# A first projection chunk computed as seven half-size products, and the modulation steps spread over other steps, in a fused two-block kernel

## The reference, cut to what matters

```python
def first_block(x, w_in, w_out, ...):
    u = einsum('bsd,de->bse', h, w_in[layer])          # 2048 -> 6752 columns
    q, k, v, z_attn, q_idx, k_idx, w_idx, z_ssd, xbc, dt_raw = _split_cols(u, IN_WIDTHS)
    ...                                                 # sparse attention, SSD mixer
    sub = einsum('bse,ed->bsd', mixed, w_out[layer])
    h = _layer_norm(DEEPNORM_ALPHA * h + sub, ln_g[layer], ln_b[layer])

def second_block(x, c, w_mod, b_mod, mod_layer, ...):
    mod = silu(c) @ w_mod + b_mod + mod_layer[l]        # one row times 2048 x 12288
    shift1, scale1, gate1, shift2, scale2, gate2 = split(mod, 6)
    ...                                                 # gating, attention, 32 experts
```

## Time and profile before

| | |
|---|---|
| median of 3 runs | 1990.54 us (1987.9 to 1991.35) |
| the profiled execution: its time, its span | 1994.43 us, 1992.7 us |
| PE busy | 1840.9 us (92%) |
| DVE busy | 1112.3 us (56%) |
| ACT, POOL busy | 321.4 us (16%), 180.4 us (9%) |
| mean granted TensorE clock | 0.984 of full |

### The profile page before, as it was taken

The page is one execution under the profiler, slowest core; times in us unless marked ns, Lnnn a source line. Parts: engine busy times, 40 slices in busy tenths (PEclk is TensorE's granted clock), DMA queues, the critical chain, the costliest instruction groups (busy, mean ns, idle before and its releaser), DMA issues.

```text
span 1992.7 us, 24068 instructions
## 1 busy us (share of the span) xinstructions
PE 1840.9 (92%) x9846; PEld 1425.9 (72%) x9846; DVE 1112.3 (56%) x1582; ACT 321.4 (16%) x607; POOL 180.4 (9%) x190
## 2 busy tenths in 40 slices
PE   8999999999999999999999999999959987788776
PEld 3788988888688788788888888868845554444443
DVE  3776677643688777767785754655463322232222
ACT  0111221221311232000241112411310000000000
POOL 0000041000000000000000000000002211111211
PEclk9999999999999999999999999999969999999999
DMA  9554532222223556568555751054299999999996
GB/s 349 184 186 154 178 122 75 79 65 84 85 85 127 192 188 242 210 232 299 185 183 201 252 192 64 22 206 169 107 376 400 409 403 403 415 404 402 413 418 242
DMA packets 153228, 448.42 MB, mean 225 GB/s; under 512 B 19446, under 2 KB 118108, under 8 KB 126748
## 3 DMA queue, kind: packets, MB, share of 16 engines
q1 hardware_dynamic: 122012, 305.92, 40.3%
q0 software_dynamic: 24288, 118.32, 17.1%
q10 hardware_dynamic: 6816, 22.60, 3.1%
HBM read 440.42 MB, written 26.28 MB: 234 GB/s over the span
## 4 chain that ended last, share of the span: by engine, by line
PE 38%; DMA 20%; DVE 3%; issue 1%; ACT 0%; POOL 0%; DVEq 0%; POOLq 0%; SPq 0%; ACTq 0%
PE bank L1184 20%; DMA RW<-in_gate_up 9%; PE bank L1213 7%; PE bank L1380 3%; DMA RA<-xn_d,dt_ 3%; DMA RX<-in_gate_up 2%; DMA RG<-in_down 2%; DMA RM<-in_down 2%; PE bank L1391 2%; PE bank L1121 1%; DMA out<-RA,dt_ 1%; PE bank L934 1%; DVE RG L1996 1%; PE bank L1007 1%; DMA RG<-in_w_mod 1%
## 5 line engine op out<-in xcount | busy, mean ns | idle before, releaser
L1184 PE MATMUL bank<-RW,RX 128*128 128x256 f32 x1792 | 404.0, 383 | 4.8 <-PE bank L1184 2.1
L1184 PEld LDWEIGHTS bank<-RW,RX 128*128 128x128 f32 x1792 | 341.7, 192 | 61.4 <-issue 14.8
L1996 DVE SCALAR_TENSOR_TENSOR RG<-RG,ccol 128x2048 f32<-128x2048 f32 x90 | 211.6, 2352 | 91.9 <-DMA RG<-in_w_mod 85.0
L1987 DVE TENSOR_TENSOR RW<-RW 128x2048 f32<-128x2048 f32 (+1 forms) x84 | 188.3, 2247 | 90.9 <-PE bank L1184 65.1
L1184 PE MATMUL bank<-RW,RM 128*128 128x256 f32 x1056 | 236.6, 380 | 1.5 <-PE bank L1184 1.2
L1184 PEld LDWEIGHTS bank<-RW,RM 128*128 128x128 f32 x1056 | 199.6, 190 | 32.1 <-issue 5.5
L2978 DVE TENSOR_TENSOR RA<-RA,bank 128x128 f32<-128x128 f32 x34 | 9.8, 288 | 282.8 <-ACT RA L1956 282.6
L1451 ACT ACTIVATE RA<-bank 128x512 f32<-128x512 f32 (+3 forms) x155 | 79.0, 538 | 539.6 <-PE bank L1184 273.3
L852 POOL DMA_DIRECT2D RG<-in_w_mod x96 | 51.3, 534 | 986.5 <-DVE RG L1996 598.9
L1184 PE MATMUL bank<-RX,RW 128*128 128x256 f32 x544 | 122.3, 379 | 0.3 <-PE bank L1184 0.3
L1184 PEld LDWEIGHTS bank<-RX,RW 128*128 128x128 f32 x544 | 102.2, 190 | 15.0 <-issue 1.6
(11 more groups left out here) (295 smaller groups left out, 2328.7 us busy)
## 6 DMA issues: line engine op xcount, KB each, us to landing
RG<-in_w_mod POOLq DMA_DIRECT2D x96, 1024.0 KB, 5.5
RW<-in_w_in SPq DMA_DIRECT2D x71, 1024.0 KB, 5.4
RX<-in_gate_up SPq DMA_DIRECT2D x22, 2048.0 KB, 42.1
RW<-in_gate_up SPq DMA_DIRECT2D x22, 2048.0 KB, 41.0
RG<-in_down SPq DMA_DIRECT2D x11, 2048.0 KB, 42.2
RM<-in_down SPq DMA_DIRECT2D x11, 2048.0 KB, 41.0
RM<-in_gate_up SPq DMA_DIRECT2D x10, 2048.0 KB, 42.4
RH<-in_gate_up SPq DMA_DIRECT2D x10, 2048.0 KB, 43.4
```

What stands on the lines that cost most here:

```text
L1184: ins = nc.tensor.matmul(bk[:, part], x, y, start=name not in ("M2", "M3") and k + j == 0, stop=k == half - 1, skip_group_check=True)
L1987: st.do(v.tensor_tensor(dst, x, y, op), s, n)
L1996: st.do(v.scalar_tensor_tensor(out=dst, in0=x, scalar=sc, in1=y, op0=op0, op1=op1), s, n)
```

## The change

Chunk 0 joins `FAST` and `project_first` goes. ACT issues all four parts of the input, by quadrants: tokens 0 to 255 of the first 4 and the next 4 blocks of features (A11), then tokens 256 to 511 of all 16 (A21 and A22, 2 MB, semaphore `x_later_tokens`), then A12. Each piece is now rows of 1 KB. DVE begins with `sum_first_input`: S1, the first weight sum of chunk 0, S2, S4, S3; its nine first mods go to later steps. The mods are distributed anew (24 before chunk 5 as before; 9, 8 and 7 in chunks 12, 13 and 14 in place of 10, 10 and 6; 6 at the end of chunk 18 in place of 4), and four of the vectors' sums on PE move: (2, 10), (12, 12), (14, 11) and (16, 11) become step 14 of the same chunk.

```diff
-        FAST_X, FAST_OUT = [1, 2, 3] + list(range(first["z"], first["za"] + 2)), [first["out"] + n for n in range(3)]
+        FAST_X, FAST_OUT = [0, 1, 2, 3] + list(range(first["z"], first["za"] + 2)), [first["out"] + n for n in range(3)]
...
-        MODS_AT = {(c, kt): 1 for c, steps in ((1, (7, 8, 9, 10, 12)), (2, (7, 8, 10, 12)), (3, (7, 8, 9, 10, 12, 13)),
-                                               (12, (0, 1, 2, 3, 4, 7, 9, 11, 13, 15)), (13, (0, 1, 2, 3, 4, 9, 10, 11, 13, 15)))
+        MODS_AT = {(c, kt): 1 for c, steps in ((0, (6, 7, 8, 9, 10, 12)), (1, (7, 8, 9, 10, 12, 13)), (2, (7, 8, 10, 12, 15)), (3, (7, 8, 9, 10, 11, 12, 13)),
+                                               (12, (0, 1, 2, 5, 7, 9, 11, 13, 15)), (13, (0, 1, 2, 3, 4, 9, 11, 13)), (14, (3, 6, 7, 9, 10, 11, 12)))
...
-        MODSUM_AT = {(2, 10): 0, (12, 12): 1, (14, 11): 2, (16, 11): 3, (19, 2): 4}
+        MODSUM_AT = {(2, 14): 0, (12, 14): 1, (14, 14): 2, (16, 14): 3, (19, 2): 4}
...
-                if n == 2:
-                    sp.dma_start(X[:, 8:KD, :], a["xt"][:, 8:KD, :]).then_inc(x_landed, 16)
...
-            act.dma_start(X[:, 0:4, :], a["xt"][:, 0:4, :]).then_inc(sem("x_first"), 16)
-            act.dma_start(X[:, 4:8, :], a["xt"][:, 4:8, :]).then_inc(sem("x_part"), 16)
+            act.dma_start(X[:, 0:4, 0:256], a["xt"][:, 0:4, 0:256]).then_inc(sem("x_first"), 16)
+            act.dma_start(X[:, 4:8, 0:256], a["xt"][:, 4:8, 0:256]).then_inc(sem("x_part"), 16)
+            act.dma_start(X[:, :, 256:S], a["xt"][:, :, 256:S]).then_inc(sem("x_later_tokens"), 16)
+            act.dma_start(X[:, 8:KD, 0:256], a["xt"][:, 8:KD, 0:256]).then_inc(x_landed, 16)
...
+            def sum_first_input():
+
+                dve.wait_ge(sem("x_later_tokens"), 16)
+                tt_(left(0, "S1"), left(0, "A21"), left(0, "A22"), ALU.add, sem("left_sums"))
+                dve.wait_ge(sem("x_first"), 32)
+                first_sum(0)
+                dve.wait_ge(sem("x_part"), 16)
+                dve.wait_ge(sem("left_sums"), 1)
+                tt_(left(0, "S2"), left(0, "S1"), left(0, "A11"), ALU.subtract, sem("left_sums"))
+                dve.wait_ge(x_landed, 16)
+                st.settle()
+                sum_left_rest(0)
+                dve.wait_ge(sem("csil_ready"), 1)
```

More of the change, by code:

```diff
@@ L466, in posts @@
             return []
-        MODS_AFTER_SUMS, MODS_AFTER_FIRST, MODS_AHEAD_OF_ROWS, MODS_BEHIND_ROWS = 7, 2, 2, 2
-        MODS_AT = {(c, kt): 1 for c, steps in ((1, (7, 8, 9, 10, 12)), (2, (7, 8, 10, 12)), (3, (7, 8, 9, 10, 12, 13)),
-                                               (12, (0, 1, 2, 3, 4, 7, 9, 11, 13, 15)), (13, (0, 1, 2, 3, 4, 9, 10, 11, 13, 15)))
+        MODS_AHEAD_OF_ROWS, MODS_BEHIND_ROWS = 2, 2
+        MODS_AT = {(c, kt): 1 for c, steps in ((0, (6, 7, 8, 9, 10, 12)), (1, (7, 8, 9, 10, 12, 13)), (2, (7, 8, 10, 12, 15)), (3, (7, 8, 9, 10, 11, 12, 13)),
+                                               (12, (0, 1, 2, 5, 7, 9, 11, 13, 15)), (13, (0, 1, 2, 3, 4, 9, 11, 13)), (14, (3, 6, 7, 9, 10, 11, 12)))
                    for kt in steps}
-        MODS_AT.update({(c, kt): 2 for c, steps in ((14, (7, 9, 12)), (15, (2, 7, 9, 12)), (16, (2, 7, 9, 12)), (19, (3, 7, 9, 12)), (20, (2, 7, 9, 12)))
+        MODS_AT.update({(c, kt): 2 for c, steps in ((15, (2, 7, 9, 12)), (16, (2, 7, 9, 12)), (19, (3, 7, 9, 12)), (20, (2, 7, 9, 12)))
                         for kt in steps})
-        MODS_AT.update({(18, 15): 4})
-        MODS_BEFORE_Z = MODS_AFTER_SUMS + MODS_AFTER_FIRST + sum(n for (c, _), n in MODS_AT.items() if c < Z_AT)
-        MODSUM_AT = {(2, 10): 0, (12, 12): 1, (14, 11): 2, (16, 11): 3, (19, 2): 4}
+        MODS_AT.update({(18, 15): 6})
+        MODS_BEFORE_Z = sum(n for (c, _), n in MODS_AT.items() if c < Z_AT)
+        MODSUM_AT = {(2, 14): 0, (12, 14): 1, (14, 14): 2, (16, 14): 3, (19, 2): 4}
         MODSUM_TILE = {}
@@ L1136, in project @@
                     beside(c, kt)
[L1138 to L1160, removed]
             def project_seven(c):
@@ L1173, in project_seven @@
                             pe.wait_ge(sem("sums_moved"), 2)
-                    if name in ("M1", "M2", "M3"):
+                    if (c, name) == (0, "M1"):
+                        pe.wait_ge(sem("x_first"), 32)
+                    elif name in ("M1", "M2", "M3"):
                         s, count = load_of[c, q]
                         pe.wait_ge(w_landed[s], count)
+                    if (c, name) == (0, "M2"):
+                        pe.wait_ge(x_landed, 16)
                     elif name in ("M5", "M6", "M7"):
@@ L1180, in project_seven @@
                     for k in range(half):
+                        if (c, name, k) == (0, "M1", 4):
+                            s, count = load_of[c, q]
+                            pe.wait_ge(sem("x_part"), 16)
+                            pe.wait_ge(w_landed[s], count)
                         for j in range(2):
@@ L1844, in stage @@
                         continue
+                    if c == 0:
+                        copy_product(c, "M1", raw(c, 0, 1))
+                        copy_product(c, "M5", raw(c, 1, 1))
                     if chunks[c][0] == "xbc" and c in FAST:
@@ L2815, in stage @@
                         mod_steps(MODS_AT.get((c, kt), 0))
-                    if c and c + 1 in FAST:
+                    if c + 1 in FAST:
                         first_sum(c + 1)
@@ L2830, in stage @@
                     elif chunks[c][0] == "xbc":
+                        if c == 0:
+                            take_pack()
                         work(c)
```

23 lines of the change are left out of this document (8 added, 15 removed).

## The result

The changed kernel takes 1994.32 us (median of 20 runs, 1989.48 to 1997.14) for 1989.99 us before (20 runs, 1987.65 to 1992.32): ratio 1.0020, interval 1.0014 to 1.0026. It is slower by about 4 us, where 2 us less were forecast. In a second comparison (12 runs beside 35 of before) the ratio was 1.0001, interval 0.9989 to 1.0012, which does not meet the first. Both together, each weighted by its interval, give about 3 us (an estimate). The profiled execution took 1992.22 us, span 1990.5, 2.2 us less than the profiled one of before. This pair points the other way because of its first member: the profiled execution of before, 1994.43 us, lies above every one of those 20 (of the 35 of the second comparison some reach 1996.18).

A forecast was written before the change was run, and what follows sets the result against it. PE's timeline was taken as the bound where the change works. Terms +1.5 - 3.1 + 1.0 + 0.9 - 3.7 + 0.6 + 1.0 gave -1.8, taken as -2 on 1994.43; less 3.9, 1988.5 us, range 1983 to 1994.5.

The forecast's parts named there:

- The base of the sum: Whole kernel: -2 us taken on the profiled 1994.43, then 3.9 taken off to reach the median of the runs: 1988.5.
- the zero for chunks 1 to 3: Chunks 1 to 3, one more mod each: no cost, with 0 to 2 us for chunk 3.
- Each stop of 1.79 us or more: PE's stops from chunk 12 on: each cost its own length and 1.7 us more through the halved clock.
- After 1.50 us of idling: PE's idling of 1.50 us, spread over more: no fall of the clock behind it, granted clock 1.00.
- Chunk 0: Start of the kernel: seven products save about 6.3 us, lost in the wait for later tokens; +1.5 us.
- Chunk 12: Chunk 12: -3.1 us from M3's stop, +1.0 for stops ahead of PV, +0.9 for clock falls behind them.
- Chunk 13 and the start of 14: Ahead of M5 of chunk 14: S1 comes earlier, saving the 2.04 us stop and 1.7 of clock; -3.7 us.
- The sums in chunks 14 and 16: PE's stops ahead of the vectors' sums: 3.3 us for 2.74 (+0.6) and 2.8 for 1.79 (+1.0).
- Rival (d): Chunk 12 stays bound by DVE's attention work, both new stops lower the clock; 1991 to 1992 us, chance 0.16.
- Rival (c): Chunk 0: later tokens land much later because quadrant rows run slower; at 250 GB/s +7, 1995.5 us; chance 0.12.
- Rival (b): Chunk 0's loads: 1 KB records run at full rate, -2.8 us more, 1985.7 us; chance 0.06.

The follow-up runs named there:

- chunk0_only: The changed kernel with the mods of chunks 12 to 18 and three of the four moved vector sums put back as before; 1995.69 us, ratio 1.0024.
- later_steps: The changed kernel with chunk 3's seventh mod at step 4, not 13, and the vector sums of chunks 14 and 16 at step 15; 1982.61 us, ratio 0.9970.
- sum_first: The changed kernel with DVE making chunk 0's first weight sum ahead of S1 instead of behind it; ratio 0.9993.
- before_again: The kernel before, without any edit, run and profiled a second time; ratio 1.0001.

## Why the prediction was wrong

**The base of the sum failed most, then the zero for chunks 1 to 3.** The step that failed most is "I take -2 on the profiled execution's 1994.43 ... That execution is 3.9 above the median". In the profiled execution all four stops of 1.79 us or more were followed by a fall of the clock, 6.8 us in all. The sum took two of those falls away as gains of the change (1.7 in chunk 12, 1.7 at the start of chunk 14), and then the 3.9 us by which the falls, in the main, had made that execution slow were taken off again: 3.4 us counted twice. "Each stop of 1.79 us or more here cost itself and 1.7 us" was read from one execution as if it were the program's. Over the profiles of all kernels here, of 14 stops of 2.53 to 3.14 us in chunks 12 to 16, 7 were followed by a fall; of 8 of 1.95 to 2.34 us, 5; of 22 of 1.72 to 1.86 us, 2. The place counts beside the length: of the 20 stops of 1.7 to 1.8 us ahead of PV one was followed by a fall, but the stop of 1.50 us ahead of chunk 18, with some 1.4 us more of idling in the 4 us behind it, was followed by one in 10 of 14 profiles, three times of 6.8 us. The prediction's "After 1.50 us of idling spread over more there was no such fall" was one execution's as well. A typical execution of before had less to give back. Its 35 runs in the second comparison say the same: the nine with a mean granted clock of 0.985 or more took 1989.0 us on average, the ten with 0.982 or less 1993.2. The Trainium skill (TensorE: Matmul & The Clock Gate, What's actually happening) says that the point at which the clock changes varies from run to run with the phase in which the first matmul lands; that the phase decides is not shown by any run here. What the profiles show is such a variation at stops in the middle of a kernel: the same stop of chunk 14 with a fall at 2.88 us in one execution and without at 2.58 in the next, and one of 3.14 us without in a third kernel.

Two more steps failed, in chunk 0 and in chunks 1 to 3. With all of them put right, the forecast's own sum is -1.8 + 3.4 (the falls counted twice) + 0.8 (chunk 0) + 1.8 (chunk 4) - 0.9 (falls in chunk 12 that did not come) = +3.3 us (an estimate), where the two comparisons together give about 3. That the profiled execution of the changed kernel took 1992.22 us, and the working had 1992.4 for it, is luck: it had falls behind both vectors' sums and behind the stop ahead of chunk 18.

**Chunk 0** (+1.5): +2.9 and +2.7 us in the two profiles of the changed kernel. With the same start chunk0_only has chunk 1 at 70.2 and later_steps at 69.2; the four average 70.3, the five profiles with the old start 68.0, which makes +2.3. So the term was 0.8 us too small. M1 at 6.6 (6.1 forecast) and the tokens near 21 (20.5) are 0.5 us late, which leaves M5 at 25.8 (25.3). The rest is the restart, which came out as 6.0, 5.6, 4.6 and 2.8 us at half rate, for 4.4. Two readings in the working are loose, without weight in the sum: by its own numbers seven products are 6.9 us less than eight, not 6.3, and two sums behind 20.5 end at 25.1, not 25.3. The record-for-record sharing of two queues was the right mechanism: from 12 to 18 us the DMA view has one record for one.

```profile
q10 hardware_dynamic: 1028, 1.05, 56.0%
q1 hardware_dynamic: 1029, 1.04, 54.2%
```

That the weight sum stands behind S1, for 2.2 us, was in the working, but not that it need not: sum_first shows it.

**Chunks 1 to 3** ("Zero, with 0 to 2 us for chunk 3, whose seventh mod stands ahead of the taking of M4"): the mechanism was named and the wrong end of its range taken. It costs 1.8 us (16.6 us for 14.7 from chunk 4's start to chunk 5's). The mods there go at the pace of their loads, and the sixth waited as long as any (3.27 us); moving one mod to step 4, as in later_steps, so that none stands at step 13, removes the stop.

**Chunk 12** (-3.1 +1.0 +0.9): the stops came as worked out, 0 ahead of M3, 1.83 for 1.8, 1.72 for 1.75. The +0.9 for falls behind the new stops was nearly nothing in fact: one fall behind the 20 stops of this kind in all kernels. Against before_again, which had no fall there, chunk 12 is 0.8 us shorter, where the terms without their falls give -0.4.

**Chunk 13 and the start of 14** (-3.7): the stop ahead of M5 of chunk 14 went, 1.5 to 2.0 us; the 1.7 for the fall was chance.

**The sums in chunks 14 and 16** (+0.6, +1.0): 2.88 and 2.58 us for 3.3, 2.75 and 2.53 us for 2.8. Against before_again's 2.06 and 2.32 that is +0.5 to +0.8 and +0.2 to +0.4. Right.

Rival (d) did not come true: M3's stop is gone, and neither of the new stops brought the clock down in either profile of the changed kernel.

**Put together** on the second profile of before: +2.7 (chunk 0), +1.8 (chunk 4), -0.8 (chunk 12), in chunk 14 -1.2 without a fall and +0.8 with one, in chunk 16 -1.4 and +0.4 (before_again had a fall there): +1 to +5 us as chance has it. The timings say +4.0 (interval 2.8 to 5.2) and +0.2 (-2.2 to +2.4). Rival (c) fell: the quadrants' rows, broken on both sides, run at the same 348 GB/s. Rival (b) fell as well. The rule by which it was worked out, 512 B for line rate in the Trainium skill (DMA: Bandwidth & Descriptors, Specifications), doesn't hold here: 348 GB/s in 1 KB records on one queue or two, 424 GB/s where 16 KB ones carry most bytes.

**Open.** In the experts' stage the time from the end of the projections to the end varies by 1 to 2 us between executions; its falls of the clock and its waits for `gate_up` were not studied. In all nine profiles with the new chunk 0 one wait there, for the transfer `RA<-xn_d`, is 2 us shorter (5.3 to 5.4 us, for 7.3 to 7.4 in the five with the old one). Some 45 us later another wait for it is 2.0 to 3.6 us, for 0.7 to 2.1, which gives part of that back; why was not tried.
